# Gate and up projections by seven half-size products, with block sums of the weights on the Pool engine

## The reference

```python
D_MODEL = 1024; SEQ = 512; DEPTH = 2
D_FF = ((8 * D_MODEL // 3 + 255) // 256) * 256      # 2816

def swiglu(h, w_gate, w_up, w_down):
    return (jax.nn.silu(h @ w_gate) * (h @ w_up)) @ w_down
...
        h = rms_norm(x, norm_ffn[i])
        x = x + swiglu(h, ffn_w_gate[i], ffn_w_up[i], ffn_w_down[i])
```

## Time and profile before

| | |
|---|---|
| median of 3 runs | 1316.63 us |
| the profiled execution | 1316.91 us |
| its span, first to last instruction | 1315.1 us |
| TensorE (PE) busy | 1295.4 us, 98% |
| weight loads (PEld) busy | 1072.1 us, 82% |
| DVE busy | 757.1 us, 58% |
| ACT busy | 521.2 us, 40% |
| Pool busy | 30.2 us, 2% |
| DMA queue of the loads | 118.89 MB, 28.3% of 16 engines |
| mean granted TensorE clock | 0.999 |

### The profile page before, as it was taken

The page is one execution under the profiler, slowest core; times in us unless marked ns, Lnnn a source line. Parts: engine busy times, 40 slices in busy tenths (PEclk is TensorE's granted clock), DMA queues, the critical chain, the costliest instruction groups (busy, mean ns, idle before and its releaser), DMA issues.

```text
span 1315.1 us, 16191 instructions
## 1 busy us (share of the span) xinstructions
PE 1295.4 (98%) x6155; PEld 1072.1 (82%) x6155; DVE 757.1 (58%) x1052; ACT 521.2 (40%) x753; POOL 30.2 (2%) x29
## 2 busy tenths in 40 slices
PE   8999999999999999999999999999999999999998
PEld 7788888888888777788888888888888878888877
DVE  6844444444447766564545444454858388888554
ACT  6442322223334555432222232333413355566434
POOL 0510000000000000000000000000000000001000
PEclk9999999999999999999999999999999999999999
DMA  5342332223242011233222222323533312113211
GB/s 191 97 128 96 96 96 96 80 71 105 88 116 81 27 65 65 65 96 96 96 96 96 96 88 72 105 88 104 163 107 128 96 33 65 40 58 129 96 65 64
DMA packets 120504, 119.54 MB, mean 91 GB/s; under 512 B 13501, under 2 KB 117385, under 8 KB 120201
## 3 DMA queue, kind: packets, MB, share of 16 engines
q1 hardware_dynamic: 120400, 118.89, 28.3%
q10 hardware_dynamic: 56, 0.01, 0.0%
HBM read 114.70 MB, written 4.19 MB: 90 GB/s over the span
## 4 chain that ended last, share of the span: by engine, by line
PE 89%; DVE 6%; ACT 2%; issue 1%; DMA 0%; DVEq 0%; SPq 0%; ACTq 0%
PE psum L1944 27%; PE psum L1946 26%; PE psum L1945 26%; PE psum L2128 1%; PE psum L2151 1%; PE psum L2313 1%; ACT w_hi L665 1%; PE psum L2285 1%; PE psum L2297 1%; PE psum L2138 1%; DVE w_lo L1174 1%; PE psum L1982 1%; PE psum L2439 1%; PE psum L1962 0%; DVE du L1512 0%
## 5 line engine op out<-in xcount | busy, mean ns | idle before, releaser
L1944 PE MATMUL psum<-xg_hi,w_hi 128*128 128x512 f32 x1088 | 432.3, 397 | 1.6 <-ACT du L1022 0.9
L1946 PE MATMUL psum<-xg_hi,w_lo 128*128 128x512 f32 x1088 | 424.0, 390 | 0.0
L1945 PE MATMUL psum<-xg_lo,w_hi 128*128 128x512 f32 x1088 | 423.7, 389 | 0.0
L1944 PEld LDWEIGHTS psum<-xg_hi,w_hi 128*128 128x128 f32 x1088 | 204.6, 188 | 44.6 <-issue 2.8
L1946 PEld LDWEIGHTS psum<-xg_hi,w_lo 128*128 128x128 f32 x1088 | 204.2, 188 | 43.1
L1945 PEld LDWEIGHTS psum<-xg_lo,w_hi 128*128 128x128 f32 x1088 | 204.5, 188 | 41.0 <-issue 1.2
L1308 DVE TENSOR_TENSOR w_lo<-w_raw,w_hi 128x2048 fp32r<-128x2048 f32 x40 | 91.8, 2295 | 145.6 <-ACT w_hi L758 145.6
L1335 DVE TENSOR_TENSOR w_lo<-w_raw,w_hi 128x2048 fp32r<-128x2048 f32 x32 | 73.4, 2293 | 115.5 <-ACT w_hi L784 115.5
L1944 PE MATMUL psum<-act_hi,w_hi 128*128 128x512 f32 x352 | 137.2, 390 | 0.0
L1945 PE MATMUL psum<-act_lo,w_hi 128*128 128x512 f32 x352 | 137.0, 389 | 0.0
L1946 PE MATMUL psum<-act_hi,w_lo 128*128 128x512 f32 x352 | 136.9, 389 | 0.0
(11 more groups left out here) (376 smaller groups left out, 1600.3 us busy)
## 6 DMA issues: line engine op xcount, KB each, us to landing
w_raw<-in_ffn_w_gate SPq DMA_DIRECT2D x22, 1024.0 KB, 5.2
w_raw<-in_ffn_w_up SPq DMA_DIRECT2D x22, 1024.0 KB, 5.1
w_raw<-in_w_in SPq DMA_DIRECT2D x16, 1024.0 KB, 5.4
w_raw<-in_ffn_w_down SPq DMA_DIRECT2D x16, 768.0 KB, 4.1
w_raw<-in_ffn_w_down SPq DMA_DIRECT2D x16, 640.0 KB, 4.0
w_raw<-in_mla_w_o SPq DMA_DIRECT2D x4, 1024.0 KB, 4.7
w_raw<-in_w_out SPq DMA_DIRECT2D x4, 1024.0 KB, 4.9
w_raw<-in_w_ple_gate SPq DMA_DIRECT2D x4, 1024.0 KB, 5.0
```

The source lines that it names most:

```text
L1944: pe.matmul(o, wh, xh, start=start, stop=False, skip_group_check=True)
L1945: pe.matmul(o, wh, xl, start=False, stop=False, skip_group_check=True)
L1946: return pe.matmul(o, wl, xh, start=False, stop=stop, skip_group_check=True)
```

## The change

In each layer the first turns stay as they were (`PLAIN`: 3 in layer 0, 2 in layer 1). The others (8 and 9, called pairs here, since each makes a pair of 128-feature tiles of gate and of up) use the Strassen-Winograd scheme: the weights of a pair are cut into 2x2 blocks (row: which of the two 128-feature tiles; column: which half of the 8 K-tiles), the tokens into 2x2 blocks (half of the features by half of the 512 tokens), and seven block products take the place of eight. A product `q` (0 to 6) is run for gate and for up (`g` = 0, 1): 4 K-tiles x 3 matmuls of 256 columns, so 14 of them and 168 matmuls a pair.

- The token terms (four sums `t1` to `t4` and three blocks) are made once a layer by DVE from `xT`, already scaled by gain and `rstd`, and split by ACT and DVE, 7 blocks of 128x1024.
- The weight side of a pair is seven blocks of 128x1024 (gate and up together): blocks 0, 1 and 5 are raw, blocks 2, 3, 4 and 6 are sums or differences that Pool makes, four `tensor_tensor` operations of 128x1024 a pair. ACT makes the high part of all seven (`block_hi`), DVE the low part (`block_lo`), into a ring of seven half-block slots in `w_hi` and `w_lo`. `w_sum`, where Pool writes blocks 4 and 6, lies in the memory of `w_lo`.
- PSUM: products 0, 2 and 4 accumulate in bank 4 and ACT copies that bank three times (`keep`, 128x512); DVE adds the kept copy and another bank to each of the four output parts (`part`, 128x512, one input in PSUM, one in SBUF). ACT applies SiLU to both gate tiles at once, DVE multiplies (128x1024). The splitting of these products into `act_hi` and `act_lo` is moved to the end of the loop (`turned_hi`, `turned_lo`, 11 of each, 128x1024).
- A unit is loaded by four DMAs of 256 KB with 512 contiguous bytes a row, in place of one of 1024 KB with 1024 bytes; SP waits for Pool's third and fourth sum of the pair before, instead of for `w_lo`.

The core of the diff, beginning with the loads on SP:

```diff
+                def load_blocks(p, col):
+                    for row in (1, 2):
+                        for g, src in enumerate((gv, uv)):
+                            dst = raw_block(l, row, col)[:, g, :].rearrange("p (k c) -> p k c", c=P)
+                            sp.dma_start(dst, src[:, 4 * col - 4:4 * col, bass.ds(p * 256 + P * (row - 1), P)]).then_inc(raw_sem[(n0 + col - 1) % 2], 16)
...
+                with sp.Fori(PLAIN[l] + 1, PAIRS) as p:
+                    for col in (1, 2):
+                        sp.wait_ge(sem("weight_sums"), sum_count(l, p, 2 + col - 4))
+                        load_blocks(p, col)
```

The counts:

```diff
+        def slots_freed(l, p, q):
+            if 2 * q + 1 >= 7:
+                return fast_count(l, p, 2 * q + 1 - 7)
...
+            return fast_count(l, p, 2 * q + 1 + 7 - 14)
```

Pool (`sq_pair` holds block 3, `second_sum` block 2; `slots_freed` is the count of finished products from which a block's ring slots are free):

```diff
+                def block_sum(p, n):
+                    if n == 1:
+                        for j in range(2):
+                            u = n0 + 2 * PLAIN[l] + j
+                            pool.wait_ge(raw_sem[u % 2], p * 64 + (loaded(u) - 64 * PLAIN[l]))
...
+                        pool.tensor_tensor(sq_pair[:, :, :], raw_block(l, 2, 1), raw_block(l, 2, 2), ALU.add).then_inc(sums, 1)
+                    elif n == 2:
...
+                        pool.wait_ge(sums, sum_count(l, p, 1))
+                        pool.tensor_tensor(second_sum[:, :, :], sq_pair[:, :, :], raw_block(l, 1, 1), ALU.subtract).then_inc(sums, 1)
+                    elif n == 3:
+                        pool.wait_ge(sem("blocks_lo"), block_count(l, p, 0))
+                        pool.wait_ge(gu, slots_freed(l, p, 4))
+                        pool.tensor_tensor(block_source(l, 4), raw_block(l, 1, 1), raw_block(l, 2, 1), ALU.subtract).then_inc(sums, 1)
+                    else:
+                        pool.wait_ge(sem("blocks_lo"), block_count(l, p, 5))
+                        pool.wait_ge(gu, slots_freed(l, p, 6))
+                        pool.wait_ge(sums, sum_count(l, p, 2))
+                        pool.tensor_tensor(block_source(l, 6), raw_block(l, 1, 2), second_sum[:, :, :], ALU.subtract).then_inc(sums, 1)
```

A steady pair on ACT:

```diff
+                def block_hi(p, q):
+                    act.wait_ge(gu, slots_freed(l, p, q))
+                    if q < 2:
...
+                        act.wait_ge(raw_sem[n % 2], p * 64 + (loaded(n) - 64 * PLAIN[l]))
+                    elif q != 5:
+                        act.wait_ge(sem("weight_sums"), sum_count(l, p, {2: 2, 3: 1, 4: 3, 6: 4}[q]))
+                    for g, dst in ring_blocks(w_hi, l, q):
+                        hi = act.activation(dst, block_source(l, q)[:, g, :], ACT.Copy)
+                    hi.then_inc(sem("blocks_hi"), 1)
+                def fast_turn(p, first=False, last=False):
+                    if not first:
+                        pair_silu(p - 1)
+                    block_hi(p, 3)
+                    keep(p, 0, 1)
+                    block_hi(p, 4)
+                    block_hi(p, 5)
+                    keep(p, 1, 5)
+                    block_hi(p, 6)
...
+                        block_hi(p + 1, 0)
+                    keep(p, 2, 9)
+                    if not last:
+                        block_hi(p + 1, 1)
+                        block_hi(p + 1, 2)
```

A steady pair on DVE, in its order (`part` waits for the number of products named, `multiply` for SiLU):

```diff
+                def fast_turn(p, first=False, last=False):
+                    if not first:
+                        part(p - 1, "c12")
+                    block_lo(p, 2)
...
+                        multiply(p - 1, p + (silu_count(l, f"pair{PLAIN[l]}") - PLAIN[l] - 1))
+                    block_lo(p, 3)
+                    part(p, "c11")
+                    block_lo(p, 4)
+                    block_lo(p, 5)
+                    block_lo(p, 6)
...
+                        block_lo(p + 1, 0)
+                    part(p, "c22")
...
+                        block_lo(p + 1, 1)
+                    part(p, "c21")
```

TensorE:

```diff
+        PRODUCTS = (("x11", 4, True), ("x21", 5, True), ("t2", 4, False), ("t1", 6, True), ("t3", 4, False), ("t4", 7, True), ("x22", 6, False))
...
+                def fast_turn(p, first=False):
+                    kept, added = sem("products_kept"), sem("parts_added")
+                    for q in range(7):
+                        pe.wait_ge(sem("blocks_lo"), block_count(l, p, q))
...
+                        if q == 0 and not first:
+                            pe.wait_ge(kept, kept_count(l, p, 3 - 3))
+                        if q in (1, 3, 5) and not first:
+                            pe.wait_ge(added, added_count(l, p, {1: "c11", 3: "c12", 5: "c21"}[q]) - 4)
+                        if q in (2, 4):
+                            pe.wait_ge(kept, kept_count(l, p, q // 2))
+                        if q == 6:
+                            pe.wait_ge(added, added_count(l, p, "c22"))
+                        for g in range(2):
+                            product(p, q, g)
```

More of the change, by code:

```diff
@@ L303, in program, with fast_units, split_count @@
         unit_src[n] = [(raw(n).rearrange("p (k c) -> p k c", k=2), a["w_ple_proj_2"][0].rearrange("(k p) n -> p k n", p=P))]
-        loads = [len(unit_src.get(n, [0])) for n in range(UNITS)]
+        PLAIN, PAIRS = (3, 2), KF // 2
+        def fast_units(l):
+            return range(FIRST[f"gateup{l}"] + 2 * PLAIN[l], FIRST[f"down{l}"])
+        loads = [4 if n in fast_units(0) or n in fast_units(1) else len(unit_src.get(n, [0])) for n in range(UNITS)]
+        def split_count(n):
+            return sum(m not in fast_units(0) and m not in fast_units(1) for m in range(n + 1))
@@ new lines, in act_pair, with act_lo_pair @@
+        def act_pair(p):
+            if isinstance(p, int) and p >= 8:
+                return work[:, 2 * p - 16:2 * p - 14, :]
+            return ffn_f32[:, bass.ds(p * 2 + 28, 2), :]
+        def act_lo_pair(t):
+            return act_lo_b[:, 2 * t - 16:2 * t - 14, :] if t >= 8 else act_lo_a[:, 2 * t:2 * t + 2, :]
+        TURN_FREED = (1, 5, 7, 9, 3, 11, 13, 1, 5, 7, 9)
+        GATED = [[f"plain{i}{c}{x}" for i in range(PLAIN[l]) for c in range(2) for x in "gum"] + [f"pair{p}" for p in range(PLAIN[l], PAIRS - 1)]
+                 + [f"lo{t}" for t in range(6)] + [f"pair{PAIRS - 1}"] + [f"lo{t}" for t in range(6, 11)] for l in range(2)]
@@ new lines, in ffn @@
+                fast_turn(first, first=True)
+                with act.Fori(first + 1, 9) as p:
+                    fast_turn(p)
+                fast_turn(9)
+                fast_turn(10, last=True)
+                down_hi(0)
+                for t in range(2, 6):
+                    turned_hi(t)
+                down_hi(1)
+                turned_hi(6)
+                pair_silu(10)
+                for t in range(7, 10):
+                    turned_hi(t)
+                down_hi(2)
+                turned_hi(10)
@@ new lines, in ffn @@
+                fast_turn(first, first=True)
+                with dve.Fori(first + 1, 9) as p:
+                    fast_turn(p)
+                fast_turn(9)
+                fast_turn(10, last=True)
+                turned_lo(2)
+                part(10, "c12")
+                down_lo(1)
+                for t in range(3, 6):
+                    turned_lo(t)
+                multiply(10, silu_count(l, "pair10"))
+                turned_lo(6)
+                turned_lo(7)
+                down_lo(2)
@@ L1326, in ffn @@
+                for t in range(8, 11):
+                    turned_lo(t)
+                down_lo(3)
                 if l == 0:
```

423 lines of the change are left out of this document (323 added, 100 removed).

## The result

The changed kernel takes 1358.03 us (median of 4 runs, 1355.85 to 1359.63) against 1316.68 us; the ratio is 1.0312, 95% interval 1.0299 to 1.0325. It is 41 us slower; forecast were 33 (1350 us, range 1314 to 1388). The profiled execution's span is 1355.3 us against 1315.1.

A forecast was written before the change was run, and what follows sets the result against it. TensorE bound the kernel before, the ring would after: first pairs 41.2 plus 15 at 24.1 make 402.7 against 370.1, +32.6. With 1 for entry and exit, +33.5 on 1316.9 gives 1350 us, range 1314 to 1388.

The forecast's parts named there:

- TensorE's pace: In gate/up pairs: 168 matmuls of 256 columns at 0.1197 us each, 20.11 us a pair against 21.77 a turn before.
- A Pool sum of 128x1024: Each of Pool's four weight sums in a pair takes 2.45 us, between 2.30 and 2.59; 9.8 us a pair.
- The exclusion: A DVE operation with two SBUF inputs and a Pool sum exclude each other for a whole instruction; path needed 19.6 us a pair.
- The ring: In steady pairs, waits from sum 4 through reload, sums and low parts to the next sum 4: 24.1 us; chance 0.64 with D.
- rival C: TensorE's clock falls after its 3 us wait: +21 us, 1371; if for whole pairs, 1600 and over; chance 0.12.
- What makes TensorE wait ahead of product 4: In steady pairs TensorE waits some 3 us before block 2's product, for DVE's low part 2.
- The entry: Entry to the pairs and exit cost 1 us for both layers, 1 to 3 a layer if cover fails; first pairs 20.6 us.
- A: Pool and DVE don't exclude each other at this size: pairs 21.5 to 22.0 us, 1311 to 1319 us; chance 0.10.
- B: TensorE stays the bound in the pairs: 1290 us; Pool's sum would have to take 1.9 us; chance 0.14.
- D: In the pairs each hand-over to Pool costs more, four at 0.3 us: +1.2 a pair, 1368 us; chance within the ring's 0.64.

The follow-up runs named there:

- experiment 7: Against experiment 5's kernel with sums on DVE: part c21 ahead of sums 1 and 2, layer 0's token terms t3 and t4 made later; 1292.71 us.
- experiment 1: Changed kernel, but after each layer's first pair DVE's weight low parts read their first operand from zeroed PSUM instead of SBUF; 1334.26 us.
- experiment 3: Changed kernel, but after each layer's first pair TensorE runs 20 unneeded 128x256 matmuls just ahead of its wait for block 2; 1350.03 us.
- experiment 2: Changed kernel, but after each layer's first pair each of a unit's four DMAs brings 64 KB instead of 256 KB; 1328.1 us.
- experiment 5: ACT's layer 0 sines moved from the first pair into the last plain turn: against experiment 4, 1300.75 us; against the changed kernel, 1355.16 us.
- experiment 6: Changed kernel with sums 1 and 2 moved to DVE, sums 3 and 4 left on Pool; 1333.92 us.
- experiment 4: Changed kernel with all four sums of a pair moved from Pool to DVE; 1303.91 us.

## Why the prediction was right

**TensorE's pace** (0.1197 us a matmul, 20.11 us a pair): right, shown in the pairs after and by experiment 7.

**A Pool sum of 128x1024** (taken 2.45, bounds 2.30 and 2.59): 2.40 us alone. From 512 to 1024 elements the time grew from 1.295 to 2.40 us, less than twice. The estimate by half of the figure in the Trainium skill (GPSIMD Engine Reference, section 3.1), 2.25 us, was 6% lower than the measurement.

**The exclusion**, read from three overlaps with Pool operations of 128x512: right at 1024, and shown by experiment 1, which changed only where the low parts read one operand (and so their values).

**The ring**, 24.1 us a pair: right as a mechanism; its terms were partly off. Against the timeline above: load with SP 6.1, measured 6.46 (5.8 to 6.7 in the steady pairs); sum 1 2.45, 2.40; low 1 and sum 2 3.67, 3.30; sum 3 2.45, 2.39; low 2 to low 5 6.8, 6.66 with the 0.28 of waiting in it, and 6.3 in the pair without a fall; sum 4 2.45, 2.39; and 0.2 from low 5 to sum 4. An operation that waited for the path ends 1.08 to 1.09 us after it is free, not 1.22, and DVE's operations follow each other at 1.14. That makes 23.4 us, and pairs without a fall of the clock take 23.2 to 23.4, the last one of layer 1 23.7. The other 0.4 to 1.1 us, in ten of the 15, are the clock's.

That the total came so near is luck in part. The 15 steady pairs took 356.0 us where 361.5 were forecast, 5.5 less: the ring was 0.7 us too long each time, and the clock, left out of the sum, gave a part of it back. The two first pairs took 49.0 us where 41.2 were forecast, 7.8 more. Errors of opposite sign leave 2.3 us.

**The clock** (rival C, 0.12): I made it an alternative to the ring; it is a consequence of it, for it follows TensorE's wait ahead of product 4 (2.2 to 2.7 us), in 10 of 14 cases. Priced were 21 us; experiment 3 took 8 off. The scatter goes with it: the four runs of the changed kernel had mean clocks of 0.985, 0.984, 0.982, 0.981 and took 1355.85, 1357.27, 1358.8, 1359.63 us, in that order, where the kernel before scatters by 0.5 us.

**What makes TensorE wait ahead of product 4**: I named low part 2. It ended at 181.98; ACT's copy of bank 4 (L958, `keep`), behind high 2, SiLU and high 3 on ACT, ended at 182.02, and the trace names it. Both come from sum 2's end, one by DVE and one by ACT, and are 0.04 us apart; my working had only the one. Where experiment 1 freed low part 2, the copy went on holding TensorE for 1.0 to 1.9 us. In a pair without a fall the ring runs through low parts 2 to 5 and not through the copy; in the ten with one it runs through TensorE's slower products, which start when the copy is done.

**The entry** (1 us for both layers, bound 1 to 3 a layer, and 20.6 us for a first pair) was mis-sized: 3.9 us in the plain turns of layer 0, 5.2 in its first pair and 2.6 in that of layer 1. I had set the token terms beside DVE's free 12 us a turn by sum, not by due time: TensorE waited 1.9 us for a gate tile behind them, then ran 3.4 us at the lower clock. That fall is not certain: in five other runs (experiments 1, 2, 5 with its two kernels, and 6) the same wait of 1.9 to 2.0 us had none behind it, and the first pair began some 2 us earlier. And I passed over ACT's sines, which stood in the first pair of layer 0 (4.1 us ahead of product 12). In layer 1 TensorE waited 2.8 us ahead of the first pair's product 4: DVE still had low parts of the token terms and the last plain tile to do, and Pool's first three sums each held an operation of DVE there (low part 1 took 2.44 us, one of a token term 3.41, the multiply of 128x512 2.21 instead of 0.69).

The profiled run took 40.4 us more than the one before, 6.9 above the 33.5 forecast. Of these, 2.3 are in the pairs (34.9 against 32.6), 2.9 in the plain turns (3.9 against 1.0), 1.2 ahead of the first feed-forward and behind the second (0.4 and 0.8, where I had put nothing, and for which I have no cause), and some 0.5 in small differences. The median lies another 0.8 above the profiled run.

**Rivals.** A (no exclusion) fell with the first timeline; what it would have given, 21.5 to 22.0 a pair, is what experiment 1 measured (21.8 to 22.1), so the ring's working was sound in that also. B needed sums of 1.9 us; they are 2.40 on Pool and 1.23 on DVE, and with those B is what happened (experiments 4 and 7). D (dear hand-overs to Pool) was there in part: from low part 5 on DVE to sum 4 on Pool it is 0.23 us (235.54 to 235.77), where ACT to DVE took 0.03; but from the last landing to sum 1 it is some 0.1, from sum 1 to sum 2 0.08, and sum 3 follows sum 2 at once. That is some 0.4 us a pair, not 1.2, and no run varied it.

## What to carry to other kernels

Handing work to an idle engine is worth nothing in itself: Pool was idle 98% of the time and DVE 42%, yet the sums belonged on DVE, since there they are twice as fast and exclude nobody. Before moving work, close the ring: follow a buffer from its release through reload, every operation and every queue it passes, back to its release, and compare that length with the bound engine's turn; here 23.4 against 20.1 us, with no engine over 65% busy beside TensorE. If a change makes TensorE wait for 2 to 3 us at regular intervals, add what its clock may cost, here 8 us. And before a difference of 2 or 3 us between two kernels is put down to an edit, compare the places of the falls of the clock in both traces: half and more of experiment 5's 3.2 us was such a fall.

## What the runs showed of the hardware that I had not expected

- TensorE's granted clock fell to the lower level for 3.4 us behind waits of 2.2 to 2.7 us in 10 of 14 cases, in experiment 1 behind the five of 1.7 to 1.9 us and behind none of the nine of 1.0 to 1.6; in experiment 2, with waits of 0.9 us at most in the steady pairs, never.
- The length of a wait alone does not settle it. Behind the same wait of 1.9 to 2.0 us in the plain turns the clock fell in three of eight traces, and behind the 2.8 us in the first pair of layer 1 in experiment 1 but not in the changed kernel.
- Twenty useless matmuls in each wait made the kernel 8 us faster.
- Behind four DMAs of 256 KB with 512-byte rows, sum 1 starts 5.7 to 6.5 us after the first is issued (6.29 in the timeline), where one DMA of 1024 KB takes 5.2; with 64 KB each sum 1 waits 3.6 to 3.8 us behind sum 4 instead of 5.8 to 6.7.
- Of two Pool operations behind each other, the second waiting for the first, the second starts 0.08 us after the first ends.
